# Hybrid four-group block, layer projections: gate slots and two rotated slots ahead of the scan

## What is computed

```python
px = (h_x * (1.0 + ca_x) + sa_x) @ w_in[l]          # combined input projection
(qa, ka, va, qb, kb, vb, qc, ic, fcf, fcb, gc, qd, kd, vd) = split(px)
o_a = window_attn(rope2d(qa), rope2d(ka), va)
o_b = global_attn(rope2d(rms(qb)), rope2d(rms(kb)), vb)
f   = lb + (1 - lb) * sigmoid(fcf or fcb)           # forget gates, two directions
o_c = hgrn_scan(silu(qc), 1 - f, ic, log f)         # forward and backward, chunked
o_d = neighbourhood_attn(qd, kd, vd)
h_x = layer_norm(ALPHA * h_x + ga_x * (concat(o_a, o_b, o_c, o_d) @ w_out[l]))
```

## Time and profile before

| | |
|---|---|
| median of 3 runs | 2174.01 us (2171.15 to 2176.42) |
| the profiled execution | 2184.93 us |
| its span | 2183.1 us |
| granted TensorE clock over the span | 0.93 |
| PE busy | 1991.6 us, 91% |
| weight loads (PEld) busy | 1701.3 us, 78% |
| DVE busy | 1400.0 us, 64% |
| POOL busy | 998.0 us, 46% |
| ACT busy | 823.7 us, 38% |
| HBM read and written | 171.00 MB, 4.19 MB |
| chain that ended last | PE 64%, DVE 16%, POOL 7%, issue 7%, ACT 3%, DMA 2% |

### The profile page before, as it was taken

One profiled execution on the slowest core, in us unless ns is written; L12 is line 12 of the kernel. 1 busy time (PEld: TensorE's weight loads), 2 busy tenths in 40 slices (PEclk: granted clock), 3 DMA queues, 4 the chain that ended last, 5 costly groups with the idle time before them and its releaser, 6 DMA issues.

```text
span 2183.1 us, 32973 instructions
## 1 busy us (share of the span) xinstructions
PE 1991.6 (91%) x12812; PEld 1701.3 (78%) x12812; DVE 1400.0 (64%) x2711; ACT 823.7 (38%) x1584; POOL 998.0 (46%) x750
## 2 busy tenths in 40 slices
PE   6898988989998899999989998798898988999997
PEld 3678988867787788888878878697886776888786
DVE  3229988775586998999943362897877672222444
ACT  2233524346633222222243343342445633333442
POOL 1236755520154464333353334675624257655543
PEclk7998977999998889999999999887899999999999
DMA  7450100120021332333321121111030112222321
GB/s 319 174 193 21 40 21 20 40 112 2 21 78 39 116 116 100 130 118 116 116 78 68 49 97 59 39 40 39 21 131 2 40 58 77 97 97 97 116 87 68
DMA packets 26938, 177.31 MB, mean 81 GB/s; under 512 B 2720, under 2 KB 3744, under 8 KB 7712
## 3 DMA queue, kind: packets, MB, share of 16 engines
q1 hardware_dynamic: 22544, 157.90, 19.8%
q10 hardware_dynamic: 4240, 17.30, 2.0%
HBM read 171.00 MB, written 4.19 MB: 80 GB/s over the span
## 4 chain that ended last, share of the span: by engine, by line
PE 64%; DVE 16%; POOL 7%; issue 7%; ACT 3%; DMA 2%; DVEq 0%; SPq 0%; POOLq 0%; ACTq 0%
PE PS L1145 22%; PE PS L1070 17%; PE PS L830 5%; PE PS L836 4%; PE PS L1006 3%; PE PS L1031 3%; DVE W L1508 3%; PE PS L990 2%; PE PS L1126 1%; DVE W L1793 1%; DVE U L1694 1%; PE PS L921 1%; POOL WL L2087 1%; PE PS L996 1%; DVE W L1724 1%
## 5 line engine op out<-in xcount | busy, mean ns | idle before, releaser
L1145 PE MATMUL PS<-XH,WS 128*128 128x512 f32 x2016 | 551.8, 361 | 11.8 <-POOL WS L2128 10.8
L1145 PEld LDWEIGHTS PS<-XH,WS 128*128 128x128 f32 x2016 | 365.4, 192 | 69.7 <-POOL WS L2128 7.6
L1145 PE MATMUL PS<-XL,WS 128*128 128x512 f32 x1008 | 362.4, 359 | 0.0
L2128 POOL TENSOR_TENSOR WS<-WR,WS 128x1024 fp32r<-128x1024 f32 x88 | 213.9, 2434 | 321.0 <-ACT WS L1363 320.7
L1432 ACT ACTIVATE W<-PS,PR 128x768 f32<-128x768 f32 (+1 forms) x88 | 78.0, 886 | 451.3 <-PE PS L1145 389.1
L1985 DVE SCALAR_TENSOR_TENSOR W<-PS,PR,W 128x511 f32<-128x511 f32 (+1 forms) x132 | 83.0, 656 | 215.0 <-ACT W L1432 215.0
L1145 PEld LDWEIGHTS PS<-XL,WS 128*128 128x128 f32 x1008 | 194.0, 192 | 27.6
L1508 DVE SCALAR_TENSOR_TENSOR W<-WR,SC,W 128x256 f32<-128x256 f32 x336 | 201.4, 641 | 6.0
L836 PE MATMUL PS<-EU,XH 128*128 128x256 f32 x624 | 194.9, 312 | 6.9 <-issue 6.3
L2087 POOL TENSOR_TENSOR WL<-WR,EU 128x512 fp32r<-128x512 f32 x96 | 126.5, 1339 | 140.7 <-ACT EU L1205 140.6
L836 PE MATMUL PS<-WL,XH 128*128 128x256 f32 x624 | 190.4, 305 | 0.0
(11 more groups left out here) (218 smaller groups left out, 4482.7 us busy)
## 6 DMA issues: line engine op xcount, KB each, us to landing
WR<-in_weights SPq DMA_DIRECT2D x134, 1024.0 KB, 4.8
U<-in_weights SPq DMA_DIRECT2D x10, 1024.0 KB, 6.9
U<-in_bias ACTq DMA_DIRECT2D x2, 1792.0 KB, 10.2
H<-in_x SPq DMA_DIRECT2D x1, 2048.0 KB, 10.7
H<-in_x ACTq DMA_DIRECT2D x1, 2048.0 KB, 15.2
U<-in_ln_rows ACTq DMA_DIRECT2D x2, 1024.0 KB, 4.3
WR<-in_weights SPq DMA_DIRECT2D x4, 512.0 KB, 3.6
kept<-H ACTq DMA_DIRECT2D x4, 512.0 KB, 2.6
```

The costliest lines, as they stand in the source:

```text
L1145: mm = pe.matmul(PS[u.pos][:, lo:hi], w[:, part, k, :], src[:, k, lo:hi], start=(k == 0 and src is xh3 and part == 0), stop=(k == KT - 1 a ...
L2128: pool.tensor_tensor(ws5[:, u.c % 2, 1], half_slot(u), ws5[:, u.c % 2, 0], ALU.subtract).then_inc(w_low, 1)
```

## The change

`ORDER` has QB and KVB behind IC, ahead of FCF. Everything up to FCF (QC, GC, IC, QB, KVB) and both gate slots FCF and FCB whole are now in front of the scan. QA, KVA, VD, QD and KD stay beside it, spread evenly over units 1 to 24, so that of layer 0's units 0, 1, 4, 7, 11, 14, 18 and 21 have no job, and of layer 1's 0, 1, 3, 5, 8, 10, 13, 15, 17, 20 and 22. DVE and POOL rotate and take roots in front too, and the fourth place of the ring moves to columns of U that are free there. The diff, whole:

```diff
--- before.py
+++ after.py
@@ -44,7 +44,8 @@
     return [("tok", p, 0) for p in range(2 + ctx)]
 
 
-ORDER = (QC, GC, IC, FCF, FCB, QA, KVA, QB, KVB, VD, QD, KD)
+ORDER = (QC, GC, IC, QB, KVB, FCF, FCB, QA, KVA, VD, QD, KD)
+OWN = ORDER.index(FCF)
 PIECES = 4
 
 
@@ -52,17 +53,17 @@
 
     whole = lambda s: [(("in", l, s, 0), p) for p in slot_parts(l, s)]
     gate = whole(FCF)
-    own = whole(QC) + whole(GC) + whole(IC)
+    own = [p for s in ORDER[:OWN] for p in whole(s)]
     extra = [(("mod", 0, i, 0), ("mod", i, 0)) for i in range(MOD_FIRST, 24)] if l == 0 else []
     mixed, n = own[:1], len(own) - 1
     for k, part in enumerate(own[1:]):
         mixed += [part] + extra[k * len(extra) // n:(k + 1) * len(extra) // n]
-    mixed += gate[:2]
-    back = whole(FCB)
-    rest = [p for s in ORDER[5:] for p in whole(s)]
-    beside = {-2: gate[2:3], -1: gate[3:4], 0: back[:2], 1: back[2:3], 2: back[3:4]}
+    mixed += gate
+    mixed += whole(FCB)
+    rest = [p for s in ORDER[OWN + 2:] for p in whole(s)]
+    beside = {-2: [], -1: [], 0: []}
     units = 4 * NT
-    first = 3
+    first = 1
     m = units + 1 - first
     for i in range(m):
         beside[first + i] = rest[i * len(rest) // m:(i + 1) * len(rest) // m]
@@ -78,10 +79,10 @@
             first.setdefault(ORDER.index(key[2]), i)
     behind, late = {}, {}
     starts = [n for n, (key, _) in enumerate(own) if key[0] == "in"]
-    for at in range(4):
+    for at in range(OWN + 2):
         opening = [n for n in starts if own[n][0][2] == ORDER[at]][0] + (at == 0)
         behind[opening] = at + 1
-    for at in range(5, len(ORDER)):
+    for at in range(OWN + 3, len(ORDER)):
         begin = first[at - 1] + (ORDER[at] == QD)
         for q in range(PIECES):
             late.setdefault(begin + q // 2, []).append((at, q))
@@ -245,7 +246,7 @@
         vlat = U[:, 7680:7680 + KT * SEQ].rearrange("p (k t) -> p k t", k=KT)
         vctx = U[:, 11776:11776 + KT * CTX].rearrange("p (k t) -> p k t", k=KT)
         lnp_mixer = x3[:, :, SEQ:TOK]
-        places = [WR[:, r * SLOT:(r + 1) * SLOT] for r in range(RING)] + [U[:, 17920:17920 + SLOT]]
+        places = [WR[:, r * SLOT:(r + 1) * SLOT] for r in range(RING)] + [U[:, 3072:3072 + SLOT]]
 
         pair = lambda e, at: e[:, at:at + 512].rearrange("p (c n) -> p c n", c=2)
 
@@ -1678,6 +1679,8 @@
                         mod_out(0, n, mod_bank(n)[:, 256:260])
                     if j.is_e:
                         forget(j)
+                    if j.rope:
+                        rotate(j)
                     if j.slot == GC:
                         dve.wait_ge(job_act, j.after[0])
                         for i in range(2):
@@ -2034,9 +2037,11 @@
                     low_weights(l, 0, q)
                 low_acts(l, 0)
                 low_acts(l, 1)
-                for n in sorted(splits[l][0]):
-                    for q in range(PIECES):
-                        low_weights(l, splits[l][0][n], q)
+                for n, j in enumerate(own_of[l]):
+                    if n in splits[l][0]:
+                        for q in range(PIECES):
+                            low_weights(l, splits[l][0][n], q)
+                    head_roots([j] if j.kind != "mod" else [])
                 pool.wait_ge(mod_done, mods_done(l))
                 for i in range(-3, len(us)):
                     if 0 <= i + 3 < len(us):
```

## The result

| | before | with the change |
|---|---|---|
| median of 4 runs | 2173.17 us (2171.15 to 2176.42) | 2188.81 us (2186.3 to 2193.7) |
| the profiled execution | 2184.93 | 2186.3 |
| its span | 2183.1 | 2184.5 |
| granted TensorE clock | 0.93 | 0.93 |
| PE busy | 1991.6 | 1978.6 |

The ratio is 1.0073, with a 95% interval of 1.0052 to 1.0095: **slower by 0.7%, 15.6 us**. The forecast was 2159, and its range ended at 2186.

A forecast was written before the change was run, and what follows sets the result against it. PE bounds layer 0's front; in the scan plain units are near balance between PE and DVE, while rotations or forget gates hang on DVE. Layer 0 -10.5 and layer 1 -4.6, together -15 from 2174, gave 2159 us; range 2146 to 2186.

The forecast's parts named there:

- Layer 0's terms: Layer 0: front +49.8, filling +12.5, scan -67.1, KD1 moved ahead of unit 23 -5.7; sum -10.5 us.
- the filling: Layer 0, before the first map: PE has nothing to do for 15.9 us instead of 3.4, +12.5.
- products that no longer wait for their slots: Layer 0's front: modulation products stand one behind a job, so PE's 4.8 us wait goes, with slow clock -5.5.
- the scan term: Layer 0's scan to unit 23: 269.6 us falls to 202.5, -67.1.
- The profiled execution lies 11 us above the median of the runs, which I carry over: Whole kernel: the 2183.1 us profiled span becomes a base of 2174, from which the 15 us gain is taken.
- POOL is mostly idle there, so I take the lower part, 4: Layer 1's front: stall from rotations and roots, bounded by 0 and 14 us, taken as 4 within +53.
- the bound of 14: Layer 1's front: the upper stall, if both QB rotations take 12.8 us on DVE against 5.9 on PE.
- rival 2: Fronts: rotations are not hidden, layer 1 loses 10 us more and layer 0 about 3; 2172, no change; chance 0.17.
- Sum 154 for 203.6: Layer 1's scan: units 4 to 11 take 77 us, 12 to 15 17, 16 to 22 60; -49.6.
- the pair: Scans: a unit without a job and the next cost about 18.2 us, since DVE works ahead.
- rival 1: Scans: pairs with an empty unit cost 20.2 us each, eleven add 22; 2181, slower; chance 0.2.
- the state-only units: Layer 1's scan, units 12 to 15, without rotations: between 14 and 27 us, taken as 17.

The follow-up runs named there:

- Turned_order: The whole change, with layer 1's front slots reordered so one without rotation stands between QB and KVB and behind KVB; 2179.68 us, ratio 1.0016 against before.
- filled: The whole change plus filler: behind 17 units without a job PE runs half the next job's products, later overwritten; 2171.29 us, ratio 0.9982 against before.
- packed: The whole change, with the jobs beside the scan one behind each unit from unit 2 and the last units empty; 2169.50 us, ratio 0.9974 against before.

## Why the prediction was wrong

- **Layer 0's terms** stand against the profile that they were counted from: front, filling, scan and end each within 3.5 us, -11.0 in sum for -10.5. The mechanisms named there (15.9 us of idle PE at the filling, measured 15.3; products that no longer wait for their slots) were right. Against the second profile of before the layer gains only 3.4, and the scan term is 7.9 too large; the lengths forecast for the changed kernel were right (202.5 us of scan, measured 205.7), the length subtracted from was not.
- **"The profiled execution lies 11 us above the median of the runs, which I carry over"** failed. I treated 11 us as lying around the stretches in question; 7.5 of them lay inside layer 0's. The change was measured against a long draw of the very rows it removes. That is 7.5 of the 29.8, and the close agreement in layer 0 is partly the luck of using that same profile twice.
- **Layer 1's front, "POOL is mostly idle there, so I take the lower part, 4"** failed: the bound of 14 was the measured case (53 + 10.4). The mean idle time of POOL said nothing; its low parts came at the moment of the roots, which rival 2 had named. Turned_order makes that front 7.8 shorter. The rival was right in layer 1 (10 more, it said), and wrong in layer 0, where modulation products stand between the jobs and PE has no wait for a transpose.
- **Layer 1's scan, "Sum 154 for 203.6"**, was mis-sized: 162.8, and behind it 14.7 where I had left 10.4. The term that failed is above all the pair. I priced an empty unit and the next at 18.2 because "DVE works ahead". In layer 0 they cost 18.3 on the mean (109.9 for six), in layer 1 19.4 (116.7 for six), near the 19.6 at which rival 1 was to decide. That is 7.5 of layer 1's 13.1 (8.8 in the scan, 4.3 behind it); 2.4 lie in the state-only units, 19.4 for 17, and the rest in single units. And 18.2 was no floor: with the filler a pair takes 16.0 in layer 0 and 17.9 in layer 1. I had booked the clock's price as a property of the units, and not as something that the spacing of the jobs makes.
- **Rival 1** gave 2181 and was nearest in time; its pairs explain some 8 of the 29.8 (7.5 in layer 1, 0.7 in layer 0). The result is rival 2's cost and part of rival 1's, both in layer 1, on a base 7.5 too long. I had given them as alternatives, and no case in which they add.
- **What the two halves are worth together** was priced nowhere. With the rotated slots in front, the gates' part costs layer 1 12.2 us in front and filling and gives 1.5 in the scan. The forecast's first part had said that "a job taken out of one of those gives little back", of plain units near balance.
- **"The trace agrees for this one"**, said of the rule of the Trainium skill, "TensorE: Matmul & The Clock Gate", section "HAM oscillation — how this bites in real kernels", that an array left idle between bursts is throttled again and pays the return every time, holds beyond the pair of the earlier trace rows: all twelve jobs behind an empty unit ran long, by 0.7 to 2.2 us. What a pair costs as a whole still lay between 16.2 and 21.2.

What stays open: in a pair, how much is the slow clock and how much the wait for DVE's copies. Over the twelve pairs filled is 23 us shorter, and 11 of them lie in the jobs themselves (17 above full clock in the change, 6 in filled). In the pair shown the job and the outputs ahead of it give 3.1 us, the wait 3.1, and one of DVE's operations in that wait (L1773) is stretched from 0.28 to 2.31 beside POOL. The filler changes all three at once. Nor was it tried to give QB's roots to an engine other than POOL.

## What to carry to other kernels

When PE's work beside a paced loop is thinned out, the place of what is left matters more than its amount: put the jobs one behind another and leave the empty units in a row. A unit without a job followed by one with a job took 18.9 us on the mean here; in packed the empty units of a row take 7.1 and most units with a job about 9. Try a change by halves and by layer before adding them up; two harmless halves lost 15 us here, and the two halves each in the right layer won 15. And take two profiles of the kernel before: a long draw may sit in the rows that the change removes, where it will be counted as gain.

## What the hardware showed that was not expected

- Up to 48 us of useless matmuls made the program 17.5 us shorter; up to 97 us still left it no longer than without. The 48 are an estimate, 17 times the 2.9 us of half a job at full clock.
- A granted clock of 0.54 over 49.6 us showed no cost where no job stood (packed, units 16 to 22, 7.1 us each), while 0.78 over the same units in the change, four of them with a job, went with 62.5 us. The clock of a window says nothing without what PE had to do in it.
- Two multiplications of DVE with both inputs in SBUF took 2.94 us beside POOL's L2092 (1.3 to 1.5 us each) and 0.76 without it. One operation of 64 columns, with one input in SBUF and one in PSUM, took 2.31 for 0.28 beside L2076 (2.34 us). In both cases the short operation took about as long as the one of POOL beside it.
